# Who turns the gathered rows and the gated product in the expert loop of a two-layer diffusion trunk

## The reference

```
g_sel = argmax(t @ w_group + b_group)              # one of 4 groups
top_w, top_i = top_k(softmax(e_logits of g_sel), 2) # 2 of its 4 experts
for e in range(16):
    a, b = split(t @ w_up[e], 2)                    # 1024 -> 512 + 512
    y = y + combine[:, e:e+1] * ((silu(a) * b) @ w_down[e])   # 512 -> 1024
x = LayerNorm(alpha * x + gate * y)
```

## Time and profile before

| | |
|---|---|
| median of 3 runs | 1293.75 us (1291.36 to 1295.17) |
| the profiled execution | 1286.74 us, its span 1284.9 us |
| PE busy | 1191.6 us, 93% of the span |
| PEld, DVE, ACT, POOL busy | 708.2, 525.7, 310.7, 166.7 us |
| read from HBM | 302.05 MB |
| expert loop of layer 0, layer 1 | 375.9 to 684.7, 963.1 to 1261.6 us of the span |

### The profile page before, as it was taken

How to read it: one execution, slowest core, us unless ns; L and a number is a source line. 1 busy time by engine, 2 the same in 40 slices (tenths; PEclk the granted TensorE clock), 3 DMA queues, 4 the chain that set the end, 5 groups by cost and what they waited for, 6 DMA issues and landing times.

```text
span 1284.9 us, 29972 instructions
## 1 busy us (share of the span) xinstructions
PE 1191.6 (93%) x12606; PEld 708.2 (55%) x12606; DVE 525.7 (41%) x1322; ACT 310.7 (24%) x637; POOL 166.7 (13%) x203
## 2 busy tenths in 40 slices
PE   4999999999999999999986999999999999999993
PEld 1455555556555565555554555466555565666551
DVE  2522223355553444343435200175663434444445
ACT  4111111200232222222223000154232222222223
POOL 0300000031001111111110100045001111111112
PEclk8799999999989999999997999989989999999997
DMA  9928878870259989245399632433055899999402
GB/s 326 392 102 288 301 268 299 299 295 8 92 230 389 409 323 410 79 166 196 120 408 391 212 105 91 149 106 98 2 185 192 344 368 409 381 409 409 186 0 82
DMA packets 104651, 305.80 MB, mean 238 GB/s; under 512 B 7136, under 2 KB 11424, under 8 KB 104256
## 3 DMA queue, kind: packets, MB, share of 16 engines
q1 hardware_dynamic: 98800, 298.43, 61.1%
q0 software_dynamic: 1648, 5.20, 1.4%
q10 hardware_dynamic: 4128, 1.05, 0.3%
HBM read 302.05 MB, written 2.62 MB: 237 GB/s over the span
## 4 chain that ended last, share of the span: by engine, by line
issue 45%; PE 42%; POOL 5%; DVE 4%; ACT 2%; DMA 1%; POOLq 0%; SPq 0%; ACTq 0%; DVEq 0%
PE bank L596 40%; POOL yg L551 4%; POOL P L569 1%; PE bank L1008 1%; DMA ring<-in_w_ada 1%; ACT x L1134 1%; DVE P L1681 1%; DVE st L1633 1%; PE bank L761 0%; PE bank L642 0%; POOLq L548 0%; DVE x L1452 0%; ACT tok L1119 0%; ACT arow L1051 0%; DVE hT L1463 0%
## 5 line engine op out<-in xcount | busy, mean ns | idle before, releaser
L596 PE MATMUL bank<-ring,xgT 128*32 128x256 f32 x4224 | 242.6, 381 | 13.9 <-issue 7.9
L596 PE MATMUL bank<-hT,ring 128*128 128x384 f32 x640 | 208.0, 487 | 0.1
L596 PEld LDWEIGHTS bank<-ring,xgT 128*32 128x32 f32 x4224 | 145.9, 110 | 93.5 <-issue 14.9
L596 PEld LDWEIGHTS bank<-hT,ring 128*128 128x128 f32 x640 | 121.1, 190 | 83.7 <-issue 0.8
L551 POOL TENSOR_TENSOR yg<-ysb,gate_s 128x256 f32<-128x256 f32 x132 | 93.9, 733 | 559.9 <-ACT ysb L1191 559.9
L596 PE MATMUL bank<-ring,heT 128*32 128x256 f32 x2112 | 127.6, 382 | 13.1 <-DVE heT L1615 10.6
L1613 DVE TENSOR_TENSOR he<-sa,bank 128x128 f32<-128x128 f32 x66 | 18.9, 287 | 221.5 <-ACT sa L1188 221.5
L596 PE MATMUL bank<-yg,ohT 32*128 32x256 f32 x1632 | 107.3, 391 | 1.5 <-POOL yg L551 1.5
L596 PE MATMUL bank<-tok,hot 128*32 128x256 f32 x1680 | 103.6, 379 | 0.0
L596 PEld LDWEIGHTS bank<-ring,heT 128*32 128x32 f32 x2112 | 62.2, 109 | 62.5 <-DVE heT L1615 25.8
L596 PEld LDWEIGHTS bank<-yg,ohT 32*128 32x128 f32 x1632 | 74.6, 184 | 34.4 <-issue 27.3
(11 more groups left out here) (230 smaller groups left out, 1316.3 us busy)
## 6 DMA issues: line engine op xcount, KB each, us to landing
ring<-in_moe_w_up SPq DMA_DIRECT2D x64, 2048.0 KB, 14.2
ring<-in_moe_w_down SPq DMA_DIRECT2D x32, 2048.0 KB, 19.3
ring<-in_w_ada SPq DMA_DIRECT2D x24, 2048.0 KB, 16.3
ring<-in_hy_w_in SPq DMA_DIRECT2D x6, 2048.0 KB, 16.3
ring<-in_na_w_qkv SPq DMA_DIRECT2D x6, 2048.0 KB, 20.7
ring<-in_hy_w_out SPq DMA_DIRECT2D x2, 2048.0 KB, 14.4
ring<-in_na_w_out SPq DMA_DIRECT2D x2, 2048.0 KB, 7.8
bm<-in_na_bias SPq DMA_DIRECT2D x16, 256.0 KB, 3.2
```

What stands on the lines that cost most here:

```text
L596: return nc.tensor.matmul(out, lhsT, rhs, start=first, stop=last)
```

## The change

The transposes leave TensorE. VectorE's block transpose turns each 32 by 32 block of a tensor in its place: what stands on partition 32i+a, column 32j+b goes to partition 32i+b, column 32j+a. It is no full transpose of 128x128, so the orders of the channels are altered to fit. The up matmul of strip q now takes the channels 128g + 32q + n (g from 0 to 7, n from 0 to 31) as its moving operand, eight runs of 32 columns, where it took two runs of 128; after the block transpose of `he`, `heT` has the channels in the order that `w_down`'s rows have. `tok` is written with its channels reordered (128m + 32j + p goes to 256j + 32m + p), so that the gather leaves in bank 1 what a block transpose makes into `xgT`. VectorE reads bank 1 itself; `xgs` and ScalarE's copy of it go away, and so do the semaphores `xgs_ready`, `xg_turned` and `he_turned`.

```diff
--- before.py
+++ after.py
@@ -272,8 +272,7 @@
         idxf = at("idxf", [128, 2, TT], RM + 4096)
         pos = at("pos", [128, TT, 16], RM + 4160)
         wk = at("wk", [128, 2, TT], RM + 4352)
-        xgT = at("xgT", [128, 2, 4, SLOT_TOK], RM + 5888)
-        xgs = at("xgs", [128, 256], RM + 6912)
+        xgT = at("xgT", [128, KT, SLOT_TOK], RM + 5888)
         sa = at("sa", [128, 128], RM + 7936)
         he = at("he", [128, 128], RM + 8448)
         heT = at("heT", [128, 128], RM + 8960)
...
@@ -841,11 +840,6 @@
                                       t == 0, t == TT - 1)
                     last.then_inc(S["gathered"], 1)
 
-                def turn_gathered(b=1):
-                    for c in range(2):
-                        last = nc.tensor.transpose(ps[b][:, 256 + 128 * c:384 + 128 * c], xgs[:, 128 * c:128 * c + 128], ident[:])
-                    last.then_inc(S["xg_turned"], 1)
-
                 def combine(done, end=False):
 
                     for r in range(TT):
@@ -878,19 +872,15 @@
                         for k in range(KT):
                             if k % 4 == 0:
                                 wait_piece(k // 4)
-                            w = wup[k // 4][:, k % 4, :].rearrange("p (g q n) -> p q g n", g=2, q=4)
+                            w = wup[k // 4][:, k % 4, :].rearrange("p (g q n) -> p q g n", q=4, n=32)
                             for q in range(4):
-                                last = mm(ps[0][32 * q:32 * q + 32, 0:256].rearrange("s (g n) -> s g n", g=2),
-                                          xgT[:, k % 2, k // 2, :], w[:, q, :, :], k == 0, k == KT - 1)
+                                last = mm(ps[0][32 * q:32 * q + 32, 0:256].rearrange("s (g n) -> s g n", n=32),
+                                          xgT[:, k, :], w[:, q, :, :], k == 0, k == KT - 1)
                         last.then_inc(S["up_ready"], 1)
 
                         pe.wait_ge(S["ohT_ready"], w1)
                         pe.wait_ge(S["yg_ready"], w1 * 2)
                         combine(w1 * 2 - 1).then_inc(S["combined"], 1)
-                        pe.wait_ge(S["he_ready"], w1)
-                        nc.tensor.transpose(ps[0][:, 256:384], he[:], ident[:]).then_inc(S["he_turned"], 1)
-                        pe.wait_ge(S["xgs_ready"], w1 + 1)
-                        turn_gathered()
                         pe.wait_ge(S["heT_ready"], w1)
                         wait_piece(2)
                         for q in range(4):
@@ -916,8 +906,7 @@
                 last.then_inc(spread_ready, 1)
                 pe.wait_ge(nb_ready, l + 1)
                 nb, total = groups_of(0), 0
-                pe.wait_ge(S["xgs_ready"], 1)
-                turn_gathered(0)
+                pe.wait_ge(S["xgT_ready"], 1)
                 pe.wait_ge(S["oh_ready"], 2)
                 gather()
                 pe.wait_ge(spread_evac, 4 * l + 4)
...
@@ -1150,7 +1137,8 @@
                 for h in range(2):
                     g = G_AT[f"tok{l}_{t}"] + h
                     wait_group(act, g)
-                    nc.scalar.activation(tok[:, t, h * 512:(h + 1) * 512], ps[bank_of(g)][:, :], ACT.Copy
+                    nc.scalar.activation(tok[:, t, :].rearrange("a (j m p) -> a m j p", j=4, m=KT)[:, 4 * h:4 * h + 4, :, :],
+                                         ps[bank_of(g)][:, :].rearrange("a (m j p) -> a m j p", m=4, j=4), ACT.Copy
                                          ).then_inc(evacuated[g % 8], 1)
 
             def moe(l):
@@ -1173,14 +1161,8 @@
                 act.wait_ge(spread_ready, 2 * l + 1)
                 for k in range(2):
                     nc.scalar.activation(wk_all[:, k, :], ps[6 + k][:, 0:TOK], ACT.Copy).then_inc(spread_evac, 1)
-                def gathered(n):
-                    act.wait_ge(S["gathered"], n)
-                    nc.scalar.activation(xgs[:], ps[1][:, 0:256], ACT.Copy).then_inc(S["xgs_ready"], 1)
-
-                gathered(1)
                 act.wait_ge(spread_ready, 2 * l + 2)
                 nc.scalar.activation(pos_all[:, 1, :], ps[7][:, 0:TOK], ACT.Copy).then_inc(spread_evac, 1)
-                gathered(2)
                 act.wait_ge(nb_ready, l + 1)
                 total = act.value_load(NBi[0:1, 32:33], min_val=EXPERTS, max_val=MAX_BLOCKS)
                 with act.Fori(0, total) as g:
@@ -1189,7 +1171,6 @@
                     act.wait_ge(S["y_ready"], g + 1)
                     act.wait_ge(S["yg_ready"], g * 2 + 2)
                     nc.scalar.activation(ysb[:], ps[0][:, 0:256], ACT.Copy).then_inc(S["ysb_ready"], 1)
-                    gathered(g + 3)
 
                 nc.scalar.activation(sd[:, 1, 0:1], credit[:, 7:8], ACT.Sqrt)
                 act.wait_ge(acc_ready, l + 1)
@@ -1595,9 +1576,8 @@
                 affine_b(2, rows)
 
                 def turned(n):
-                    dve.wait_ge(S["xg_turned"], n)
-                    src = ps[0 if isinstance(n, int) else 1][:, 256:512]
-                    v.tensor_copy(xgT[:].rearrange("p c j s -> p (c j s)"), src).then_inc(S["xgT_ready"], 1)
+                    dve.wait_ge(S["gathered"], n)
+                    v.transpose(xgT[:].rearrange("p m s -> p (m s)"), ps[1][:, 0:256]).then_inc(S["xgT_ready"], 1)
 
                 one_hot(1)
                 turned(1)
@@ -1611,8 +1591,8 @@
                     one_hot(g + 2)
                     dve.wait_ge(S["sa_ready"], g + 1)
                     v.tensor_tensor(he[:], sa[:], ps[0][:, 128:256], ALU.mult).then_inc(S["he_ready"], 1)
-                    dve.wait_ge(S["he_turned"], g + 1)
-                    v.tensor_copy(heT[:], ps[0][:, 256:384]).then_inc(S["heT_ready"], 1)
+                    dve.wait_ge(S["he_ready"], g + 1)
+                    v.transpose(heT[:], he[:]).then_inc(S["heT_ready"], 1)
                     turned(g + 2)
 
                     dve.wait_ge(S["srow_ready"], g + 1)
```

More of the change, by code:

```diff
@@ L348, in build @@
             moe_sems.append({n: sem(f"{n}{l}") for n in (
-                "oh_pair", "oh_moved", "oh_ready", "gathered", "xgs_ready", "xg_turned", "xgT_ready", "up_ready", "sa_ready",
-                "he_ready", "he_turned", "heT_ready", "y_ready", "ysb_ready", "yg_ready", "ohk_ready", "ohT_ready", "srow_ready", "combined")})
+                "oh_pair", "oh_moved", "oh_ready", "gathered", "xgT_ready", "up_ready", "sa_ready",
+                "he_ready", "heT_ready", "y_ready", "ysb_ready", "yg_ready", "ohk_ready", "ohT_ready", "srow_ready", "combined")})
         block = ctx.enter_context(nc.Block())
@@ L927, in moe @@
                 pe.wait_ge(S["ohT_ready"], 1)
-                pe.wait_ge(S["xgT_ready"], 1)
                 for e in range(EXPERTS):
@@ L935, in moe @@
                 combine(total * 2 + 1, True).then_inc(acc_ready, 1)
-                pe.wait_ge(S["xgs_ready"], total + 2)
             project_out(0, yT)
```

## The result

| | before | after |
|---|---|---|
| median | 1292.55 us (4 runs, 1291.33 to 1295.17) | 1255.78 us (4 runs, 1254.0 to 1260.9) |
| ratio of the runs | | 0.9719, 95% interval 0.9686 to 0.9753 |
| profiled execution: span | 1284.9 us | 1253.1 us |

A forecast was written before the change was run, and what follows sets the result against it. TensorE's own program order bounds a block, with weight DMA the limit where experts are small. Gains of 17.7 (layer 0) plus 20.1 (layer 1) less 1 (clock) make 36.8 us: 1293.75 to 1257, range 1247 to 1275.

The forecast's parts named there:

- The turns, 0.71 us a block: Between combine and down on TensorE: removing one turn of he and two of xgs saves 0.71 us in 66 blocks.
- heT is covered by combine: VectorE's transpose of he, taken as 0.29 us, ends while combine (1.58 us) runs, so it costs nothing on the path.
- xgT, ScalarE, tok: nothing: VectorE's transpose to xgT (0.43 us), ScalarE's dropped copy and tok's reordered writes: 0; tok at worst 1 us per layer.
- The switch of tiling: Combine to down: tiling change drains TensorE once instead of twice; 0.33 us idle stays in the sum, second cost unseen.
- The runs, 0 to 8 us: Up matmuls reading eight runs of 32 columns, not two of 128: taken as 0, at most 8 us in all.
- Ahead of the loops, 0.4 us each: Before each layer's expert loop: gather follows the index matmuls directly and pos_all starts earlier, worth 0.4 us a layer.
- What the weights take back: Expert weight loads limit part of the gain: layer 0 keeps 17.7 of 23.8 us, layer 1 loses 3.7, keeping 20.1.
- Clock, 1 us for all: Granted clock dropping from 2.4 to 1.2 GHz after waits on weights: 1 us lost in all, most dips swallowed.

The follow-up runs named there:

- late3: Changed kernel with three more VectorE transposes, into tensors nobody reads, ahead of the one into heT; 1270.34 us, ratio to before 0.9833.
- xg_only: Changed kernel with TensorE's turn of he, VectorE's copy to heT and the two-run order of the up matmuls put back; 1290.66 us, ratio to before 0.9998.
- he_only: Kernel before with only the product he turned by VectorE, the picked rows still turned by TensorE; 1270.27 us, ratio to before 0.9855.
- runs2: Changed kernel with up matmuls reading two runs of 128 columns again, output differs, one block less; 1250.47 us, ratio to before 0.9686.
- runs4: Changed kernel with up matmuls reading 64 runs of four columns, output differs, one block less; 1249.33 us, ratio to before 0.9674.
- stride: Changed kernel with up matmuls reading 256 single columns 16 bytes apart, output differs, one block less; 1475.04 us, ratio to before 1.1428.

## Why the prediction was right

- *The turns, 0.71 us a block.* Right: 8.83 became 8.12 in the trace, and it was 46.0 us for 64 blocks with light weights, where 64 x 0.71 is 45.4.
- *`heT` is covered by combine.* Right: the transpose takes 0.31 us, `heT` is 0.43 us early, one more transpose is free, and beyond the cover, in `late3`, what `heT` is late shows whole in the block. The Trainium skill's 311 ns ("VectorE: DVE Perf Modes", "The three transpose paths") is for 128x128 in bf16; the trace has 311 ns for fp32.
- *`xgT`, ScalarE, `tok`: nothing.* Right: 0.41 us where the copy took 0.43, and the copies into `tok` take 603 ns on average, 604 before. In `xg_only`, which has all three, the time is that of before.
- *The switch of tiling.* The weight load of down is idle for 0.33 us behind combine, as the first turn's was; it was in the sum already. What the second switch cost, which the prediction could not see, stands in `he_only`: 0.17 us between the turns and down.
- *The runs, 0 to 8 us.* 0 by the five blocks of an expert that doesn't wait, 41.1 us in `runs2`, in `runs4` and in the changed kernel.
- *Ahead of the loops, 0.4 us each.* Half of it, 0.22 us: in layer 1 from the router's spread matmuls to the first up it is 9.54 us, 9.76 before, and in layer 0 from the index matmuls to the first up 4.88, 5.10 before. The second gather starts where the index matmuls end, and `pos_all` follows those matmuls, not the turn.
- *What the weights take back.* Right in layer 0. By the rule (a release, 9.8 us to the first piece, 5.12 for each further one) the eighth piece lands 45.6 us after the eleventh expert's mark; it landed 45.7 after it. The layer was to gain 17.7 us, 17.3 of them in the loop, and gained 17.0 there. Layer 1 was to gain 19.7 in the loop and gained 17.9, and here the rule was too short: the 23rd piece was to land 122.4 us after the mark of expert 3 and landed 124.2 after it. The first piece took 10.8 us instead of 9.8, while the queue still brought the last piece of the expert before, which landed 3.1 us after the mark; the 22 further ones took 113.4 instead of 112.6. So TensorE lost 5.2 us to weights where the sum has 3.7: 3.6 in waits (0.7 of them in expert 10, counted from 0, where none was expected, and 2.9 in expert 13, where the prediction named 3 to 5) and 1.6 in a half up at 1.2 GHz. That is the term of the sum that was sized too small, by 1.5 us.
- *Clock, 1 us for all.* Two dips are in the loops, and half an up took 3.53 and 3.52 us in them instead of 1.93. The window of the first has a granted clock of 0.50, 1.2 GHz (the third number from the end):

```profile
417.41:420.69 3.28, 3.28 (x32) 1.38 (x32) 0.00 (x0) 0.00 (x0) 0.00 (x0) 0.50 1.03 412
```

Behind each dip stands a wait of only 0.15 us for the next piece. In `runs2` the same half up of expert 13 in layer 1 kept its clock (1.00), and down then waited 1.76 us:

```profile
1141.88 1.93 PE L595 MATMUL bank<-ring,xgT 128*32 128x256 f32 x32 [3.09 <-DMA ring<-in_moe_w_up]
...
1147.09 1.93 PE L595 MATMUL bank<-ring,heT 128*32 128x256 f32 x32 [1.76 <-DMA ring<-in_moe_w_down]
```

From that half up to down it is 5.19 us with the dip and 5.20 without: the next piece sets the time either way. So such a dip costs nothing of its own there, and the 1.6 us belong to the term of the weights, not beside it.

Taken together, the loops were to give 36.0 us (17.3 and 19.7, less 1 for the clock) and gave 34.9; the stretches ahead of them were to give 0.8 and gave 0.4. The mechanism was right, but that the median of the runs hit the forecast by a microsecond was luck: the two profiled executions differ by 31.8 us, the medians by 36.8.

## What to carry to other kernels

Between two long pieces of work look for all the chains that run side by side, not for the instructions: here one half of the change was worth 0.35 us a block, the other nothing, and only both together gave 0.71. Then ask what the shorter loop will be short of, and walk from one release of a buffer to the next with the transfer time; that told in advance that weights would take back some 10 of the 48 us. And when an experiment changes numbers that later decide how much work there is, compare the stage ahead of that point, or count the work.

## What the runs showed of the hardware

- VectorE's block transpose in fp32: 0.31 us for 128x128 from SBUF, 0.41 for 128x256 from PSUM (0.44 in `xg_only`), about as long as the copy (0.43). The next instruction starts 0.24 and 0.33 us after the start of such a transpose.
- A moving operand read in single fp32 columns 16 bytes apart doubles a matmul (7.42 us an up instead of 3.64, `stride`); in runs of 16 bytes it costs nothing (3.64, `runs4`).
- TensorE's weight load was idle 0.41 us ahead of combine, 0.33 behind it and 0.17 between 128x128 turns and down (`he_only`), each time at a change of the tiling, and not at all from down to gather to up, which share one.
- Pieces of 2 MB landed about 5.1 us after each other while the queue was full. The first one behind an expert's mark landed 8.2 (changed kernel) to 9.8 us (before) after the marks of the eleventh expert of layer 0, with the queue empty, and 10.8 where the queue still held a piece.
- The granted clock was at 1.2 GHz (0.50) in a half up behind waits for weights of 3.05 us before and 3.06 and 2.76 us after, and that half up took 3.34 to 3.53 us. Behind a wait of 3.09 us at the end of layer 0, and one of 3.09 us in `runs2`, it stayed at 2.4 GHz (1.00). So the length of the wait alone does not tell.
